# Down projection of parts 1 and 2 by seven products of weight quarters, with the weight sums made and stored ahead in part 1

## The chip, the cores and the metric

The kernel runs on one core of one Trainium2 chip. The metric is the time of one execution on the device in microseconds (us), as the median of several runs; lower is better. PE is the matrix engine (TensorE), DVE the vector engine, ACT the scalar engine, POOL the GpSimd engine, SP the engine that here only issues DMAs.

## What is computed

One layer of a hybrid decoder for 2048 prompt tokens and 32 sample tokens, in float32, with model width 1024 and inner width 2816 (11 x 256). What matters here is the feed-forward step:

```python
x = x + concat([h_mlstm, y_conv]) @ w_out
f = rmsnorm(x, g_ffn)
x = x + (silu(f @ w_gate) * (f @ w_up)) @ w_down     # w_down: 2816 x 1024
e = rmsnorm(pe @ w_ple, g_ple)
x = x + sigmoid(x @ w_pg) * e
```

## The kernel before

**Parts.** The 2080 tokens are worked through in three parts (q = 0, 1, 2) of 704, 704 and 672 tokens, each split in two token blocks of N = 352 or 336 columns. Every part reads every weight. A part runs the stages "in" (12 pairs of 256 output columns of w_in), "out" (4), the embedding, the feed-forward (11 pairs p of `gate` and `up`, 256 inner columns each), "pg" (4).

**Products.** A pair is a matrix of 1024 x 256 weights times 1024 x 2N activations, cut into quarters (A11, A12, A21, A22 of the weight, B11 and so on of the activations) and done by seven products instead of eight, P1 to P7, which use three of the quarters and four sums of weight quarters (S1 to S4) against four quarters and sums of the activations. Each product is 4 rows of 128 x 3 matmuls (12 in all), since a float32 product is made of high x high, high x low and low x high parts (`three`, L610). The order in a pair is P1 P6 P5 P7 P2 P4 P3. DVE and ACT add the products up from PSUM banks: P6 is added by DVE to a copy of P1 and frees its bank, which P7 needs; P7's addition frees the same bank for P4.

**Weight entries.** The weight operand of one product is an *entry*: 128 x 1024, the high part beside the low part, in one of five ring buffers (`RING`, `wring`). Entry e goes to the buffer of entry e - 5 and must wait until that has been used. An entry is either *prepared* from raw weights in SBUF (ACT copies the high part at L1287, POOL subtracts to get the low part at L2708) or *loaded* from the DRAM tensor `weight_parts` by a DMA that ACT issues (L1279). Part 0 prepares all entries, has DVE make the sums, and SP stores A11 and the sums of each pair (L1082); parts 1 and 2 load those five and prepare only A12 and A22. ACT, DVE and POOL call `ahead()` once per product, for the entry some four products later; each engine follows its own fixed program, in order, with semaphores between engines.

**Spares.** In part 0 the sums for "pg" (16 of them) are made in between as *spare* entries: SP loads a set of raw weights to `spare_raw` (L1091), DVE makes the four sums in place (`spare_sum`, L1753), ACT and POOL turn each into an entry of the ring, SP stores it, and PE passes over it. An entry of the ring that follows a spare by five waits until the spare has been stored.

**Raw weights.** SP loads raw weights two raws ahead into four buffers (`wraw`, `raw`, L1065), each when the raw four before has been prepared.

**Down.** `down(q, g)` (PE L980, DVE L2500) runs between `gate` and `up` of odd pairs and adds to x the product of the hidden pairs 2g - 1 and 2g with 512 rows of w_down, plainly: 16 products (8 output chunks of 128 by 2 token blocks) of 4 x 3 matmuls, banks 6 and 7 in turn, one DVE addition each (L2509). Its 8 entries are all prepared from raw weights. g = 0 has half a group, g = 5 the last pairs. The hidden values are split into high and low at L1580 (ACT) and L2443 (DVE): half c = 1 of a pair at its `up`'s end, half c = 0 after P1 of the next `gate`.

Of the kernel before, what the change touches and what calls it, by code (L numbers as in the profile page):

```python
# [168 lines left out]
def build(nc, x_prompt, x_sample, p_prompt, p_sample, state_C, state_n, state_m, state_conv, g_mix, w_in,  # L169
# [154 lines left out]

    def add_raw(pieces):

        r = len(raws)
# [20 lines left out]
    def add_spare(r, n):  # L348
# [6 lines left out]
        keep_entry(("pg", set_), name)  # L355
        spare_last[set_] = n_prepared[0]

    def add_pairs(q, of, members, order, spares):
# [5 lines left out]
        if stored:  # L364
            made = []
            for w, c0 in members:
                if (of[0], "A11") in kept_as:
# [4 lines left out]
                r, buf = add_raw([(slice(0, 1024), w[:, :, c0:c0 + P]), (slice(1024, 1536), w[:, 4:8, c0 + P:c0 + 2 * P])])  # L372
                v = buf[:, 0:1536].rearrange(k8, n=P)
                made.append((r, {"A11": v[:, 0:4, :], "A12": v[:, 4:8, :], "A22": v[:, 8:12, :]}, {}))
        else:
# [2526 lines left out]
```

## Time and profile before

| | |
|---|---|
| median of 3 runs | 2590.44 us (2589.56 to 2590.97) |
| the profiled execution | 2590.48 us, its span 2588.5 us |
| busy share of the span | PE 95%, weight loads 93%, DVE 58%, ACT 35%, POOL 39% |
| mean granted clock of TensorE | 0.985 of 2.4 GHz |
| DMA | 501 MB, 194 GB/s in the mean |

In the profile, a matmul's busy time overlaps the next one's, so busy PE means that matmuls follow each other; the pace of products is read from the start times of what they release. In the rows below, `<-` after a square bracket names what ended an engine's idle time. Feed-forward of part 1 runs from about 1240 to 1695 us, of part 2 from about 2080 to 2520 us.

### The profile page before, as it was taken

Reading aid. Unit: us, or ns where it says so; the run is one execution under the profiler, and the core shown is the slowest. Engines: PE = TensorE matmul, PEld = TensorE weight load, DVE = VectorE, ACT = ScalarE, POOL = GpSimd, SP = SyncE. Lnnn points to the kernel's source line nnn. Section 1 sums busy time; section 2 is a strip of 40 time slices with the busy share of each in tenths; the row PEclk is TensorE's granted clock in tenths of the full one; section 3 lists DMA queues with packets and bytes.
Section 4 is the critical chain, followed back from the end, with each engine's and each line's share of the span. In section 5 each row is a group of like instructions: output and inputs, shape, how many; then the busy total and the mean of one; then the engine's idle time right before and its main releaser. Section 6 shows DMA issues by size and latency. Waiting matters only on the chain.

```text
span 2588.5 us, 40956 instructions
## 1 busy us (share of the span) xinstructions
PE 2469.4 (95%) x15757; PEld 2404.5 (93%) x15757; DVE 1492.6 (58%) x2327; ACT 909.3 (35%) x1694; POOL 1011.0 (39%) x785
## 2 busy tenths in 40 slices
PE   7899788999999999999999999999999999999998
PEld 6888778999999989999999999998899999999997
DVE  7668987666555684477543333468457664332355
ACT  5344443343334543334312112355234431212133
POOL 4656755576666342122322122333222232322233
PEclk8999999999999999999999999999999999999999
DMA  6646644576666756575545544575657555564544
GB/s 222 218 174 236 221 150 179 192 272 220 213 229 210 228 158 205 174 268 160 179 163 195 200 142 163 179 225 179 196 183 244 184 182 171 187 219 164 173 137 149
DMA packets 285044, 501.00 MB, mean 194 GB/s; under 512 B 18428, under 2 KB 182613, under 8 KB 284343
## 3 DMA queue, kind: packets, MB, share of 16 engines
q1 hardware_dynamic: 212182, 273.59, 31.4%
q10 hardware_dynamic: 72672, 224.82, 26.2%
q8 instruction: 128, 2.10, 0.3%
q14 instruction: 62, 0.50, 0.1%
HBM read 374.70 MB, written 123.65 MB: 193 GB/s over the span
## 4 chain that ended last, share of the span: by engine, by line
PE 73%; DVE 7%; DMA 4%; issue 2%; ACT 1%; POOL 1%; DVEq 0%; ACTq 0%; POOLq 0%; SPq 0%
PE bank L612 23%; PE bank L614 22%; PE bank L613 22%; DMA wring<-weight_parts 2%; DVE qlo L1801 1%; DMA xs<-x_prompt 1%; PE bank L805 1%; DVE ess L2426 1%; PE bank L749 1%; PE bank L738 0%; POOL wring L2708 0%; DMA weight_parts<-wring 0%; PE bank L811 0%; DVE wraw L1791 0%; PE bank L727 0%
## 5 line engine op out<-in xcount | busy, mean ns | idle before, releaser
L2708 POOL TENSOR_TENSOR wring<-wraw,wring 128x512 fp32r<-128x512 f32 x525 | 768.1, 1472 | 1223.0 <-ACT wring L1287 1220.7
L612 PE MATMUL bank<-qhi,wring 128*128 128x352 f32 (+1 forms) x3540 | 1155.5, 326 | 65.2 <-DVE u L1912 13.9
L614 PE MATMUL bank<-qhi,wring 128*128 128x352 f32 (+1 forms) x3540 | 1139.5, 322 | 0.0
L613 PE MATMUL bank<-qlo,wring 128*128 128x352 f32 (+1 forms) x3540 | 1137.6, 321 | 0.0
L612 PEld LDWEIGHTS bank<-qhi,wring 128*128 128x128 f32 x3540 | 672.4, 190 | 89.7 <-issue 77.9
L613 PEld LDWEIGHTS bank<-qlo,wring 128*128 128x128 f32 x3540 | 672.4, 190 | 0.0
L614 PEld LDWEIGHTS bank<-qhi,wring 128*128 128x128 f32 x3540 | 670.0, 189 | 0.0
L1287 ACT ACTIVATE wring<-wraw 128x512 fp32r<-128x512 f32 x531 | 331.3, 628 | 710.3 <-PE bank L614 553.5
L612 PE MATMUL bank<-hid,wring 128*128 128x352 f32 (+1 forms) x1056 | 341.5, 323 | 12.4 <-DVE wide L2509 7.4
L614 PE MATMUL bank<-hid,wring 128*128 128x352 f32 (+1 forms) x1056 | 339.7, 322 | 0.0
L613 PE MATMUL bank<-hid,wring 128*128 128x352 f32 (+1 forms) x1056 | 338.9, 321 | 0.0
L2509 DVE TENSOR_TENSOR wide<-wide,bank 128x352 f32<-128x352 f32 (+1 forms) x288 | 148.0, 515 | 295.1 <-PE bank L614 295.1
L612 PEld LDWEIGHTS bank<-hid,wring 128*128 128x128 f32 x1056 | 199.9, 189 | 16.7 <-issue 13.0
L613 PEld LDWEIGHTS bank<-hid,wring 128*128 128x128 f32 x1056 | 200.8, 190 | 0.0
L614 PEld LDWEIGHTS bank<-hid,wring 128*128 128x128 f32 x1056 | 199.9, 189 | 0.0
L1862 DVE TENSOR_TENSOR u<-t,bank 128x352 f32<-128x352 f32 (+1 forms) x84 | 43.2, 514 | 187.0 <-PE bank L614 187.0
L2708 POOL TENSOR_TENSOR wring<-s,wring 128x512 fp32r<-128x512 f32 x74 | 109.3, 1489 | 64.0 <-ACT wring L1287 64.0
L1855 DVE TENSOR_TENSOR u<-t,bank 128x352 f32<-128x352 f32 (+1 forms) x87 | 44.6, 513 | 133.5 <-PE bank L614 104.4
L1580 ACT ACTIVATE hid<-sl 128x704 fp32r<-128x704 f32 (+3 forms) x69 | 52.1, 755 | 190.2 <-DVE sl L1833 183.4
L2443 DVE TENSOR_TENSOR hid<-sl,hid 128x704 fp32r<-128x704 f32 (+3 forms) x69 | 103.9, 1517 | 8.8 <-ACT hid L1580 7.4
L1316 ACT ACTIVATE t<-bank 128x352 f32<-128x352 f32 (+1 forms) x123 | 56.2, 457 | 129.8 <-PE bank L614 129.8
L1287 ACT ACTIVATE wring<-s 128x512 fp32r<-128x512 f32 x74 | 45.8, 629 | 87.6 <-PE bank L614 52.3
(322 smaller groups left out, 2413.3 us busy)
## 6 DMA issues: line engine op xcount, KB each, us to landing
wring<-weight_parts ACTq DMA_DIRECT2D x418, 512.0 KB, 4.5
weight_parts<-wring SPq DMA_DIRECT2D x201, 512.0 KB, 3.8
wraw<-w_down SPq DMA_DIRECT2D x33, 1024.0 KB, 8.3
wraw<-w_in SPq DMA_DIRECT2D x14, 1024.0 KB, 7.2
wraw<-w_gate SPq DMA_DIRECT2D x11, 1024.0 KB, 5.9
wraw<-w_up SPq DMA_DIRECT2D x11, 1024.0 KB, 6.0
wraw<-w_in SPq DMA_DIRECT2D x44, 256.0 KB, 5.2
wraw<-w_gate SPq DMA_DIRECT2D x44, 256.0 KB, 3.6
```

Of the source, the lines that this page charges most:

```text
L612: nc.tensor.matmul(o, hi, mh, start=begins, stop=False, skip_group_check=True)
L613: nc.tensor.matmul(o, hi, ml, start=False, stop=False, skip_group_check=True)
L614: return nc.tensor.matmul(o, lo, mh, start=False, stop=ends, skip_group_check=True)
L749: last = nc.tensor.matmul(bank[bk][:, a - a0:z - a0], roots[0:n, t:t + 1].to_broadcast([n, P]), ident[0:n, a - t0:z - t0], start=True, sto ...
L1287: nc.scalar.activation(whi[e % RING][:, :].rearrange("p (k n) -> p k n", k=k), w.src, ACT.Copy).then_inc(hi_done, 1)
L1316: nc.scalar.activation(t1[n % 2][:, 0:q.N], bank[a][:, 0:q.N], ACT.Copy).then_inc(free[a], 1)
L1580: nc.scalar.activation(hid[:, 0, x, blk], sl[:, c, blk], ACT.Copy).then_inc(h_hi, 1)
L1855: nc.vector.tensor_tensor(w2, t, c, add).then_inc(fc, 1)
L1862: nc.vector.tensor_tensor(w3, w2 if first else t, d, add).then_inc(fd, 1)
L2443: nc.vector.tensor_tensor(hid[:, 1, x, blk], sl[:, c, blk], hid[:, 0, x, blk], sub).then_inc(h_lo, 1)
L2509: last = nc.vector.tensor_tensor(x, x, bank[bk][:, 0:q.N], add)
L2708: nc.gpsimd.tensor_tensor(wlo[e % RING][:, :].rearrange(v, k=k), w.src, whi[e % RING][:, :].rearrange(v, k=k), ALU.subtract).then_inc(lo_d ...
```

## The change

The groups g = 1 to 4 of `down` in parts 1 and 2 are done by seven products of quarters too. Inner chunks of pair 2g - 1 against those of pair 2g are the rows, even against odd output chunks the columns of the quarters, token block 0 against 1 the columns of the activations. An entry now holds 2 x 2 chunks of weights (256 x 256), and half a group (a = 0 or 1, 512 output columns) has seven entries; each is used for two sets m of output chunks, 2 x 3 matmuls each, on all eight banks. Of the seven entries three are prepared from raw weights and four are loaded sums. The sums of the eight half groups (sets 4 to 11, 32 spares) are made in part 1 by the spares' machinery, in `up` 2 to `up` 8 (four each), `gate` 3 (two) and `down` 1 (two). The hidden pairs are kept in seven forms (B11, B12, B21, B22 and T1 to T4; high in `dhi`, low in `dlo_first`, `dlo_rest`), which takes more DVE and ACT passes per group; the raw buffers 2 and 3 give their room to them, so parts 1 and 2 have two raw buffers and SP loads a raw no longer two ahead. A cut of the diff:

```diff
+PG_SETS = 4
+DOWN_SEVEN = (1, 2, 3, 4)
+DOWN_SPARES = {("up", 2): {0: 16, 2: 17, 4: 18, 6: 19}, ("gate", 3): {4: 20, 6: 21}, ("down", 1): {1: 22, 3: 23},
+               ("up", 3): {0: 24, 2: 25, 4: 26, 6: 27}, ("up", 4): {0: 28, 2: 29, 4: 30, 6: 31},
...
+               ("up", 7): {0: 40, 2: 41, 4: 42, 6: 43}, ("up", 8): {0: 44, 2: 45, 4: 46, 6: 47}}
+DOWN_SPARE_LOADS = {25: 5, 27: 6, 29: 7, 31: 8, 35: 9, 37: 10, 41: 11}
...
+        b = r % 2 if q else r % RAW_RING
...
+            def down_by_sevens(q, g):
+                begins = ("P1", "P6", "P5", "P7", "P4")
+                for a in range(2):
+                    for name in DOWN_PRODUCTS:
...
+                        for m in range(2):
+                            first, second, third, fourth = DOWN_BANKS[m]
...
+                            for k in range(2):
+                                last = three(bank[bk][:, 0:q.N], hi[:, k, m, :], lo[:, k, m, :], dhi[:, op, k, 0:q.N],
+                                             down_low(op)[:, k, 0:q.N], name in begins and k == 0, k == 1)
...
                 for r in range(RAWS):
-                    raw()
+                    if q.n or r < RAWS - 2:
+                        raw()
...
+                    if q.n == 1 and r == 25:
+                        spare_weights(PG_SETS)
...
+                    if q.n == 1 and r in DOWN_SPARE_LOADS:
+                        spare_weights(DOWN_SPARE_LOADS[r])
...
+            def hidden_parts(q, p, c):
...
+                if p % 2:
+                    dve.wait_ge(h_hi, HID_HIGH[(q.n, p, (c, "B12"))])
+                    nc.vector.tensor_tensor(dlo_first[:, c, 0:q.N], u[:, 0], dhi[:, 0, c, 0:q.N], sub).then_inc(h_lo, 1)
+                    nc.vector.tensor_tensor(t_1, u[:, 1], u[:, 0], sub).then_inc(h_lo, 1)
+                    return
+                dve.wait_ge(h_hi, HID_HIGH[(q.n, p, (c, "B2"))])
+                nc.vector.tensor_tensor(dlo_rest[:, 0:2, c, 0:q.N], u, dhi[:, 1:3, c, 0:q.N], sub).then_inc(h_lo, 1)
...
+                nc.vector.tensor_tensor(t_2, u[:, 1], t_1, sub).then_inc(h_lo, 1)
+                nc.vector.tensor_tensor(t_3, u[:, 1], t_3, sub).then_inc(h_lo, 1)
...
+                nc.vector.tensor_tensor(t_4, u[:, 0], t_2, sub).then_inc(h_lo, 1)
```

Three places show how instructions move. In rows of the change, line numbers are those of the changed kernel (L1395 is the load L1279 of before, L1403 the ACT copy L1287).

**ACT, `up` 3 of part 1** (`wring` with a number is a ring buffer, `parts_kept` a stored part, `prod` a product of PE). Before, from the load for P1 of `up` to that for P1 of the next `gate`:

```order
L1279 DMA wring3_80<-weight_parts 128x1024 [waits parts_kept5,prod]
L1279 DMA wring4_81<-weight_parts 128x1024 [waits parts_kept1,prod]
L1279 DMA wring0_77<-weight_parts 128x1024 [waits parts_kept2,prod]
L1279 DMA wring1_78<-weight_parts 128x1024 [waits parts_kept4,prod]
L1287 ACTIVATE wring2_79<-wraw3_73 128x512 [waits landed3,prod]
L1316 ACTIVATE t1_1_114<-bank3 128x352 [waits free4,prod]
L1569 ACTIVATE sl_105<-sl_105 128x352 [waits free1]
L1287 ACTIVATE wring3_80<-wraw3_73 128x512 [waits prod]
L1279 DMA wring4_81<-weight_parts 128x1024 [waits parts_kept5,prod]
L1279 DMA wring0_77<-weight_parts 128x1024 [waits parts_kept0,prod]
```

Now, from the load for P6 of `up` to that for P1 of the next `gate`:

```order
L1395 DMA wring4_85<-weight_parts 128x1024 [waits parts_kept1,prod]
L1395 DMA wring0_81<-weight_parts 128x1024 [waits parts_kept2,prod]
L1403 ACTIVATE wring1_82<-spare_raw_78 128x512 [waits spare_sums,prod]
L1395 DMA wring2_83<-weight_parts 128x1024 [waits parts_kept4,prod]
L1403 ACTIVATE wring3_84<-wraw1_75 128x512 [waits landed1,parts_kept0]
L1403 ACTIVATE wring4_85<-spare_raw_78 128x512 [waits spare_sums,prod]
L1432 ACTIVATE t1_1_118<-bank3 128x352 [waits free4,prod]
L1700 ACTIVATE sl_109<-sl_109 128x352 [waits free1]
L1403 ACTIVATE wring0_81<-wraw1_75 128x512 [waits prod]
L1395 DMA wring1_82<-weight_parts 128x1024 [waits parts_kept5,parts_kept1]
L1403 ACTIVATE wring2_83<-spare_raw_78 128x512 [waits spare_sums,prod]
L1395 DMA wring3_84<-weight_parts 128x1024 [waits parts_kept0,prod]
```

The five buffers now also take the spares. The last load (P1 of `gate` 4) goes to buffer 3, which P2 of `up` held; between P2 and P1 PE has only P4 and P3. P7 (buffer 2) takes the place of P1, two products before it.

**DVE, from the end of an even pair's `up` into the next `gate`, part 2.** Before:

```order
L1831 TENSOR_TENSOR u2_115<-u2_115,bank4 128x336 [waits silu_done,free5,prod]
L1833 TENSOR_TENSOR sl_105<-sl_105,u2_115 128x336 [waits free4]
L2443 TENSOR_TENSOR hid_55<-sl_105,hid_55 128x672 [waits h_hi] x2
L1855 TENSOR_TENSOR u2_115<-t1_0_113,bank2 128x336 [waits h_raw,prod,free0]
L1862 TENSOR_TENSOR u3_116<-t1_0_113,bank2 128x336 [waits h_raw,prod]
```

Now (L2011 is L1855 of before, the addition of P6; L2018 is L1862, that of P7):

```order
L1987 TENSOR_TENSOR u2_119<-u2_119,bank4 128x336 [waits silu_done,free5,prod]
L1989 TENSOR_TENSOR sl_109<-sl_109,u2_119 128x336 [waits free4]
L2605 TENSOR_TENSOR dlo_rest_58<-sl_109,dhi_56 128x2x336 [waits h_hi]
L2607 TENSOR_TENSOR draw_59<-sl_109,draw_59 128x336 [waits h_lo]
L2608 TENSOR_TENSOR draw_59<-sl_109,draw_59 128x336
L2610 TENSOR_TENSOR draw_59<-sl_109,draw_59 128x336 [waits h_lo]
L2605 TENSOR_TENSOR dlo_rest_58<-sl_109,dhi_56 128x2x336 [waits h_hi]
L2607 TENSOR_TENSOR draw_59<-sl_109,draw_59 128x336 [waits h_lo]
L2608 TENSOR_TENSOR draw_59<-sl_109,draw_59 128x336
L2610 TENSOR_TENSOR draw_59<-sl_109,draw_59 128x336 [waits h_lo]
L2011 TENSOR_TENSOR u2_119<-t1_0_117,bank2 128x336 [waits h_raw,prod,free0]
L2617 TENSOR_TENSOR dlo_rest_58<-draw_59,dhi_56 128x2x336 [waits h_lo,h_hi] x2
```

Eight passes stand ahead of P6's addition where two stood.

**DVE and SP, `gate` 2 of part 1**, where the first set (set 4) comes in. DVE, from P6's addition (L2011) to P7's (L2018):

```order
L2011 TENSOR_TENSOR u2_119<-t1_0_117,bank2 128x352 [waits h_raw,prod,free0]
L2590 SCALAR_TENSOR_TENSOR wide0_49<-wide0_49,gains_131,bank7 128x352 [waits full7]
L2590 SCALAR_TENSOR_TENSOR wide0_49<-wide0_49,gains_131,bank7 128x352
L1919 TENSOR_TENSOR spare_raw_78<-spare_raw_78 128x4x128 [waits spare_in]
L2590 SCALAR_TENSOR_TENSOR wide0_49<-wide0_49,gains_131,bank7 128x352 x2
L2018 TENSOR_TENSOR u3_120<-t1_0_117,bank2 128x352 [waits h_raw,prod]
```

SP, from the raw of `gate` 3 to the load of set 5:

```order
L1181 DMA wraw0_74<-w_gate 128x4x128 [waits lo_done]
L1181 DMA wraw0_74<-w_gate 128x4x128
L1203 DMA spare_raw_78<-w_down 128x4x512 [waits full6,lo_done]
L1189 DMA weight_parts<-wring2_83 128x1024 [waits lo_done]
L1189 DMA weight_parts<-wring0_81 128x1024 [waits lo_done]
L1189 DMA weight_parts<-wring3_84 128x1024 [waits lo_done]
L1189 DMA weight_parts<-wring1_82 128x1024 [waits lo_done]
L1203 DMA spare_raw_78<-w_down 128x4x512 [waits lo_done]
```

The sum L1919 that waits for `spare_in` is new between the two additions. The load of set 5 stands behind the store of `up` 2's last spare; DVE's first sum of set 5 stands ahead of P3's additions of `up` 2.

## Rows read from the trace of the kernel before

**Rows 1.** The page's part 1, busy time by engine (us, share, instructions), and chain by engine:
```profile
PE 2469.4 (95%) x15757; PEld 2404.5 (93%) x15757; DVE 1492.6 (58%) x2327; ACT 909.3 (35%) x1694; POOL 1011.0 (39%) x785
PE 73%; DVE 7%; DMA 4%; issue 2%; ACT 1%; POOL 1%; DVEq 0%; ACTq 0%; POOLq 0%; SPq 0%
```

**Rows 2.** Waits of PE, 1274 to 1660 us (part 1): total us, times, longest:
```profile
PE bank L612 <- DVE hid L2443: 0.9, 1, 0.9
PE bank L612 <- DMA wring<-weight_parts: 0.6, 2, 0.5
```

**Rows 3.** Busy time by window: PE, PEld, DVE, ACT, POOL, clock, DMA share and GB/s:
```profile
1258.50:1272.00 13.50, 12.90 (x71) 12.89 (x72) 6.58 (x14) 0.00 (x0) 0.00 (x0) 0.87 0.41 123
1379.60:1393.10 13.50, 13.50 (x86) 13.50 (x85) 3.08 (x6) 3.40 (x7) 2.80 (x3) 1.00 0.78 273
622.00:636.00 14.00, 13.45 (x85) 13.20 (x84) 10.08 (x12) 6.46 (x11) 10.45 (x8) 1.00 0.92 317
1272.00:1658.00 386.00, 385.26 (x2411) 383.68 (x2409) 140.87 (x241) 83.27 (x142) 99.33 (x75) 1.00 0.53 177
```

**Rows 4.** Timeline, first and last addition of group 1, part 1 and part 2:
```profile
1333.73 0.52 DVE L2509 TENSOR_TENSOR wide<-wide,bank 128x352 f32<-128x352 f32 x1 [1.41 <-PE bank L614]
...
1362.38 0.52 DVE L2509 TENSOR_TENSOR wide<-wide,bank 128x352 f32<-128x352 f32 x1 [1.38 <-PE bank L614]
...
2172.09 0.50 DVE L2509 TENSOR_TENSOR wide<-wide,bank 128x336 f32<-128x336 f32 x1 [1.33 <-PE bank L614]
...
2199.73 0.50 DVE L2509 TENSOR_TENSOR wide<-wide,bank 128x336 f32<-128x336 f32 x1 [1.33 <-PE bank L614]
```

**Rows 5.** Timeline, DVE and POOL, from an `up` into a `gate`, part 2:
```profile
2321.65 1.48 POOL L2708 TENSOR_TENSOR wring<-wraw,wring 128x512 fp32r<-128x512 f32 x1 [9.05 <-ACT wring L1287]
2321.91 2.87 DVE L2443 TENSOR_TENSOR hid<-sl,hid 128x672 fp32r<-128x672 f32 x2
...
2324.48 1.45 POOL L2708 TENSOR_TENSOR wring<-wraw,wring 128x512 fp32r<-128x512 f32 x1 [1.35 <-ACT wring L1287]
2324.70 0.50 DVE L1855 TENSOR_TENSOR u<-t,bank 128x336 f32<-128x336 f32 x1
...
2328.30 0.51 DVE L1862 TENSOR_TENSOR u<-t,bank 128x336 f32<-128x336 f32 x1 [3.11 <-PE bank L614]
```

**Rows 6.** Timeline of DVE, part 1, one such pass that began with POOL idle:
```profile
1379.26 0.89 DVE L2443 TENSOR_TENSOR hid<-sl,hid 128x704 fp32r<-128x704 f32 x1 [0.56 <-ACT hid L1580]
```

**Rows 7.** Loads of stored parts, 1270 to 1660 us, and the time to landing:
```profile
L1279 ACTq DMA_DIRECT2D wring<-weight_parts x92: 326/326/327, 1270.5 to 1647.4; - x92
...
DMA to landing us min/median/max: 3.3/4.8/8.3
```

**Rows 8.** DMA issues: count, KB each, median us to landing; then landing of L1091:
```profile
wraw<-w_down SPq DMA_DIRECT2D x33, 1024.0 KB, 8.3
...
DMA to landing us min/median/max: 6.3/9.0/10.0
```

**Rows 9.** Groups of instructions, the spares of part 0 (mean ns behind the comma):
```profile
L2708 POOL TENSOR_TENSOR wring<-spare_raw,wring 128x512 fp32r<-128x512 f32 x16 | 22.9, 1429 | 19.1 <-ACT wring L1287 19.1
...
L1763 DVE TENSOR_TENSOR spare_raw<-spare_raw 128x512 f32<-128x512 f32 x16 | 15.3, 959 | 0.0
...
L1287 ACT ACTIVATE wring<-spare_raw 128x512 fp32r<-128x512 f32 x16 | 10.0, 624 | 25.5 <-PE bank L614 25.5
```

**Rows 10.** Timeline, `gate` 2 of part 1 (DVE, SP), and PE at 1259 us:
```profile
1259.10 0.40 PE L612 MATMUL bank<-hid,wring 128*128 128x352 f32 x1 [2.27 <-DVE wide L2509]
...
1294.48 0.37 SPq L1074 DMA_DIRECT2D wraw<-w_down  x1
...
1295.13 0.52 DVE L1855 TENSOR_TENSOR u<-t,bank 128x352 f32<-128x352 f32 x1 [1.82 <-PE bank L614]
1295.57 2.05 DVE L2434 SCALAR_TENSOR_TENSOR wide<-wide,gains,bank 128x352 f32<-128x352 f32 x4
1298.94 0.52 DVE L1862 TENSOR_TENSOR u<-t,bank 128x352 f32<-128x352 f32 x1 [1.32 <-PE bank L614]
```

More of the change, by code:

```diff
@@ L449, in build, with spares_of, add_down @@
     ALL4, ALL2 = slice(0, 4), slice(0, 2)
-    def add_down(g, n=None):
+    def spares_of(q, w, p):
+        return DOWN_SPARES.get((w, p)) if q == 1 else None
+    def add_down(q, g, n=None):
         if g == 0:
-            add_plain(w_down_v[:, 0:2, :], 2, D, [(ALL2, slice(256 * n, 256 * n + 256)) for n in range(4)])
+            add_plain(q, w_down_v[:, 0:2, :], 2, D, [(ALL2, slice(256 * n, 256 * n + 256)) for n in range(4)])
+            return
+        if down_seven(q, g):
+            spares = spares_of(q, "down", g) or {}
+            for a in range(2):
+                r, buf = add_raw(q, [(slice(0, 2048), w_down_v[:, 4 * g - 2:4 * g + 2, 512 * a:512 * a + 512])])
+                for j, p in enumerate(DOWN_PRODUCTS):
+                    name = WEIGHT_OF[p]
+                    if name in ("A11", "A12", "A22"):
+                        add_entry(r, by_quarters(buf)[name], 0, name == "A11")
+                        end[r] = n_prepared[0]
+                    else:
+                        n_loads[0] += 1
+                        entries.append(Entry(r, None, 0, False, None, None, kept_as[(("down", g - 1, a), name)]))
+                        entries[-1].loads = n_loads[0]
+                    if not a and j in spares:
+                        add_spare(r, spares[j])
             return
         for a in range(2):
-            add_plain(w_down_v[:, 4 * g - 2:4 * g + 2, 512 * a:512 * a + 512], 4, 512,
+            add_plain(q, w_down_v[:, 4 * g - 2:4 * g + 2, 512 * a:512 * a + 512], 4, 512,
                       [(ALL4, slice(P * j, P * j + P)) for j in range(4)], {1: n, 3: n + 1} if a and n is not None else None)
@@ L1282, in one_ahead @@
                 if w.first:
[L1283 removed]
+                    act.wait_ge(landed[raw_buffer[w.raw]], raw_landed[w.raw])
                 if w.total:
@@ L1565, in e_square, with down_by_sevens @@
                 nc.scalar.activation(esq[:, :, 0:q.T], q.U[:, 2 * x:2 * x + 2, 0:q.T], ACT.Square).then_inc(e_sq, 1)
+            def down_by_sevens(q, g):
+                n = PAIR_NO[(q.n, "up", 2 * g + 1)]
+                for a in range(2):
+                    for name in DOWN_PRODUCTS:
+                        ahead()
+                        if name != "P1":
+                            continue
+                        for m in range(2):
+                            bk, key = DOWN_BANKS[m][0], (q.n, "down", g, 2 * a + m)
+                            act.wait_ge(*written[key + ("P1",)])
+                            act.wait_ge(*drained[(q.n, "down", g, m, "P7") if a else PAIR_KEYS[n - 2 + m] + ("P3",)])
+                            nc.scalar.activation(t1[(n + m) % 2][:, 0:q.N], bank[bk][:, 0:q.N], ACT.Copy).then_inc(free[bk], 1)
+                            t_used[n + m] = key + ("P7",)
             def late_silu(q, p):
```

222 lines of the change are left out of this document (173 added, 49 removed), and 1 row of the table DOWN_SPARES.

## The prediction

> **What bounds the kernel now.** I read the busy shares and the chain first [rows 1]: PE is busy for 95% of the span and the chain of waits lies on PE for 73%. Then PE's waits in the feed-forward of part 1: in some 386 us PE waits 1.5 us in all, 0.6 us of it for loads of stored weights [rows 2]. DVE is busy 141 us of that window, POOL 99, ACT 83, and the DMA engines for 53% [rows 3]. So the stage is a nearly gapless stream of matmuls: a matmul taken out is a gain in full, and any new wait of PE is a loss in full. The question is what the new sums, stores and loads do to a ring of five buffers whose transfers only just fit now.
>
> The sum is made against the profiled execution, 2590.48 us (span 2588.5 and 2.0 around it), which is 0.04 above the median of the runs. About 0.2%, or 5.2 us, is what a measurement of this kernel can tell from no change.
>
> **The change, part by part.**
>
> *Matmuls removed.* A group took 16 x 12 = 192 matmuls and now takes 2 x 7 x 12 = 168. From the first to the last addition of a group are 15 steps of 12 matmuls: 28.65 us in part 1 and 27.64 in part 2 [rows 4], that is 0.1592 and 0.1536 us per matmul. Four groups a part, 24 each: 96 x 0.1592 = 15.3 us and 96 x 0.1536 = 14.7 us. Together -30.0 us.
>
> *DVE inside `down`.* Half a group has 18 additions where it had 8, 18 x 0.52 = 9.4 us [rows 4] in a half of 13.4 us (seven products of 1.91). They bunch up at P2 (six in one product), but each bank is wanted again only several products later. Zero; the cover is the rest of the half.
>
> *Hidden pairs, the odd boundary.* After an odd pair DVE makes four passes of half the length where it had two: zero.
>
> *Hidden pairs, the even boundary.* After an even pair eight passes stand ahead of P6's addition where there were two. In part 2 DVE starts them at 2321.91 and P6's addition follows at 2324.70; P7 of `gate` was written by 2328.30, so it began at 2328.30 - 1.84 = 2326.46, and needs the bank that this addition frees [rows 5]. A pass of 704 that begins with POOL idle takes 0.89 us [rows 6], so 0.85 for 672; a pass of 336 takes 0.51 by the length of the additions. The chain is 2 x (0.85 + 3 x 0.51) = 4.76 us undisturbed: P6's addition ends at 2321.91 + 4.76 + 0.50 = 2327.17, 0.7 us late. That is the lower end. The two passes of before took 2.87 instead of 1.70, 1.2 us lost beside POOL [rows 5]; I take the same loss, so 1.9 us late. If both POOL passes (1.48 and 1.45) came whole on top, it would be 3.6; that is the upper end. Four boundaries: +7.6 us in part 2 (2.8 to 14.4). In part 1 the next `gate`'s P1 is late by the item after this one, which moves the due time by about as much: zero, up to +6. The price of the upper end is what a rule says: the Trainium skill, "SBUF — State Buffer", section "Who interferes with whom", has a DVE instruction with two SBUF inputs and a GpSimd instruction that reads SBUF exclude each other for a whole instruction. By it the even boundaries of part 2 cost 14.4 us instead of 7.6; the rows show part of that loss.
>
> *The ring in `up` 2 to `up` 8 of part 1.* Now a load is issued when the product five entries back is done, with four products between: 4 x 1.91 = 7.6 us for a landing that takes 3.3 to 8.3, median 4.8 [rows 7]; hence the 0.6 us of waits. With four spares among an `up`'s seven products two loads, those of P7 and of the next `gate`'s P1, get a buffer that was freed only two products before: 3.8 us. ACT can't issue earlier, since it waits for that buffer in its program's order. PE then waits landing - 3.8: nothing at 3.3, 1.0 us at the median, 4.5 at the longest. P7 I take at the median, 1.0. P1 of `gate` is loaded beside the spare's store, the next raw and a set of 1 MB on SP's queue; I take 5.7, between median and longest, 1.9 us. Some 2.9 us an `up`, seven times: +20.3 us (ends 0 and 63; I use 8 to 35, since few of the 92 landings were near either end at once). `gate` 3 and `down` 1 with two spares each have one such load: +2 (0 to 4).
>
> *Set 4, DVE in `gate` 2.* The first sum of set 4 stands between P6's and P7's additions. SP issues the set after the raw of `gate` 3, which waits for `gate` 2's last preparation; that event was at 1294.48 [rows 10]. Two issues later, 1295.4, the load starts; 1 MB of w_down lands in 8.3 us in the median, the sets of part 0 took 6.3 to 10.0 [rows 8]. At 1303.7 DVE makes the sum (0.96 [rows 9]), two scalings (4 took 2.05) and P7's addition (0.52): 1306.2. P7 was written at 1298.94 and P4, one product later (1300.85), needs its bank: PE waits 5.4 us (3.4 to 7.1). After an idle time of 2.27 us the granted clock was 0.87 over 13.5 us [rows 3, 10], 1.8 us lost at the lower of the two levels (1.2 GHz); I add that once. +7.2.
>
> *Set 5, DVE at the end of `up` 2.* Its load waits for `up` 2's last spare, whose buffer P7 of `up` 2 frees, 8.0 us into the pair; ACT 0.62, POOL 1.43 [rows 9], then the store is issued: 10.2. Landed at 18.5, and only then come the sum (0.96), P3's two passes (1.05), the eight passes (4.9 undisturbed), the next sum (0.96) and P6's addition of `gate` 3 (0.52): 26.9. P7 of `gate` 3 is due after ten products and the ring's waits, 19.1 + 2.9 = 22.0. PE waits 4.9 us (2.9 to 9.5), and 1.8 for the clock: +6.7. The later sets have seven products more, or DVE asks for them after P6's addition: zero.
>
> *Raw weights.* SP now loads each raw behind the same preparation as before but for two raws later in the order, so 9 products or more (17 us) ahead of its use against 8.3 [rows 8]: zero.
>
> Sum: part 1 -15.3 + 20.3 + 2 + 7.2 + 6.7 = +20.9; part 2 -14.7 + 7.6 = -7.1. Together +13.8: **2604 us**.
>
> **The rivals.**
>
> *The loads land in time (faster).* If landings in the `up` pairs stay near 3.3 to 4.3, the ring costs 0.5 an `up`, 3.5, and 1 at `gate` 3; the sets at their quick end cost 3.4 and 2.9 with no loss of clock. Part 1: -15.3 + 10.8 = -4.5, part 2 -7.1: 2579 us. For it: a landing alone takes 3.3, and POOL, DVE and ACT have room. Against it: the median is 4.8 with the DMA engines 53% busy, and the spares add 16.8 MB of stores, 16.8 of loads and 8.4 of sets to 386 us at 177 GB/s, 110 MB in all, 286 GB/s. It decides from a cost of about 1.1 us an `up` on. 15%.
>
> *The gain and the waits cancel.* Costs between these: 2585 to 2596. 15%.
>
> *The DMA engines become the bound.* An `up` with spares moves five loads, its raw, four stores and a set, 6.3 MB, and a `gate` 3.1: 9.4 MB in 26.7 us. The densest window moved 317 GB/s at a share of 0.92, so 345 at the most [rows 3]: 27.3 us; at 317, 29.7 us. Then landings go to the long end, about 6 us an `up` instead of 2.9: 2604 + 22 = 2626. Against it: the halves of `down` between them move less. 24%. (The Trainium skill, "DMA: Bandwidth & Descriptors", section "Specifications", gives about 358 GB/s from HBM for a core; by it the 9.4 MB take 26.3 us and this rival would not hold.)
>
> *DVE and POOL exclude each other wholly.* The upper end at the even boundaries: 6.8 us more, 2611. Against it: the two passes of before lost 1.2 us, not 2.9 [rows 5]. The rule is the one named above. 10%.
>
> That the change doesn't do what it says is excluded by the order of the instructions: the spares and the 24 matmuls less a group stand there.
>
> **How the numbers follow.** The forecast has 36% (2596 to 2612). Slower by over 0.2% (above 2595.7) is the forecast, the DMA bound and the exclusion: 36 + 24 + 10 = 70%; within 0.2% 15%; faster 15%. The range 2584 to 2632 leaves out most of the faster rival's lower half and the far end of the DMA bound, about 2 in 10.
>
> **What would show it.** In part 2 `down` groups at 2 x 7 x 1.84 = 25.8 us instead of 29.5, and four waits of PE of about 2 us for the addition of P6 (L2011) at `gate` 3, 5, 7 and 9. In part 1 waits of PE or its weight load for `wring<-weight_parts` about 15 to 25 us in all, two waits of about 5 us behind L1919 at `gate` 2 and `gate` 3, a clock under 1 behind them. The forecast is wrong if PE's waits for loads stay under 8 us, or if part 2 doesn't gain.

## The result, and the profile after

The changed kernel takes 2622.89 us in the median of four runs (2615.56 to 2628.24), the kernel before beside it 2590.70 (2589.56 to 2599.69). The ratio is 1.0118, with an interval of 1.0103 to 1.0134: slower, by some 32 us where 13.8 were forecast; the time lies inside the stated range. The profiled execution is the slowest of the four, 2628.24 us with a span of 2626.5, so it shows 37.8 us to account for, 5.4 of them above the median.

The page of the changed kernel, busy time by engine and the chain [rows 1]:

```profile
PE 2460.2 (94%) x15565; PEld 2384.7 (91%) x15565; DVE 1649.9 (63%) x2615; ACT 955.8 (36%) x1790; POOL 1034.0 (39%) x801
PE 67%; DVE 9%; DMA 7%; issue 3%; POOL 1%; ACT 1%; DVEq 0%; SPq 0%; ACTq 0%; POOLq 0%
```

PE lost 9 us of busy time and 192 matmuls, and the chain has moved from PE (73% to 67%) to DVE and the DMAs. PE's waits, the first three rows in the feed-forward of part 1 [rows 2], 1285 to 1670 us, the last two in that of part 2, 2145 to 2530 us (total us, times, longest):

```profile
PE bank L696 <- DMA wring<-weight_parts: 19.4, 22, 2.9
PE bank L696 <- DVE u L2011: 11.1, 4, 9.0
PE bank L696 <- DVE u L2018: 5.8, 1, 5.8
...
PE bank L696 <- DVE u L2011: 6.3, 3, 2.3
PE bank L696 <- DMA wring<-weight_parts: 3.6, 2, 3.4
```

So 36.3 us of waits stand in part 1 where 1.5 stood. Windows of the same kernel (columns as in [rows 3]): all of that stretch, a stretch with spares from `up` 3 to `gate` 5, the densest 10 us, and 10 us each behind gate 2's wait, around gate 3's, around a late load in `down` 1, and behind the waits of gates 5, 7 and 9 in part 2:

```profile
1285.00:1670.00 385.00, 348.52 (x2087) 337.96 (x2086) 221.03 (x377) 105.61 (x188) 123.24 (x91) 0.97 0.78 268
1397.36:1443.67 46.31, 42.36 (x254) 40.03 (x253) 26.50 (x41) 15.51 (x27) 15.15 (x11) 1.00 0.93 323
1440.00:1450.00 10.00, 8.89 (x55) 8.34 (x54) 7.10 (x11) 4.05 (x6) 1.29 (x1) 1.00 1.04 391
1310.00:1320.00 10.00, 10.00 (x55) 9.94 (x54) 7.04 (x15) 3.32 (x6) 3.09 (x3) 0.85 0.48 159
1340.00:1350.00 10.00, 3.44 (x12) 3.47 (x13) 8.62 (x13) 1.84 (x3) 1.74 (x2) 0.51 0.30 105
1360.00:1370.00 10.00, 7.06 (x35) 6.76 (x34) 3.91 (x8) 2.60 (x5) 3.00 (x4) 0.83 1.01 386
2286.50:2296.50 10.00, 9.95 (x65) 9.98 (x66) 5.00 (x8) 4.05 (x9) 2.59 (x2) 1.00 0.82 273
2366.60:2376.60 10.00, 9.96 (x54) 9.99 (x55) 4.99 (x8) 3.12 (x6) 1.28 (x2) 0.83 0.83 260
2448.30:2458.30 10.00, 9.93 (x55) 9.96 (x56) 5.02 (x8) 3.16 (x6) 1.29 (x2) 0.83 0.79 253
```

DVE's busy time in part 1 went from 141 to 221 us, the traffic from 177 to 268 GB/s, and the granted clock shows 1.2 GHz for part of the time behind several waits.

**Where the time went.** The time of one pair is found by subtracting the starts of P7's addition (L1862 before, L2018 now) of equal pairs. From `up` 1 to `up` 10 of part 1 these go from 1282.17 to 1651.22 us before and from 1283.72 to 1688.83 now: 405.11 - 369.05 = +36.1 us. In part 2, 2122.50 to 2478.70 against 2161.13 to 2516.96: -0.4. The rest of the program adds 2. The same subtraction for all the kernels below:

| us against before | up 2 | gate 3 | up 3 to up 10 | part 1 | part 2 | whole time, median (before beside it) |
|---|---|---|---|---|---|---|
| changed kernel | 9.7 | 13.2 | 13.2 | 36.1 | -0.4 | 2622.89 (2590.70) |
| e1, P6's addition first | 9.2 | 11.5 | 14.6 | 35.4 | -11.1 | 2612.31 (2592.07) |
| e2, set 4 earlier | 1.9 | 13.3 | 12.2 | 27.4 | -0.2 | 2612.26 (2592.07) |
| e3, spares spread | 11.8 | 13.5 | 28.6 | 53.8 | -2.5 | 2635.11 (2592.07) |
| e4, raws alone | 0.0 | 0.0 | -1.6 | -1.6 | 0.5 | 2590.91 (2592.07) |
| e5, six buffers | 7.3 | 11.6 | 0.3 | 19.2 | -2.6 | 2606.23 (2591.97) |
| e7, six buffers, spread | 5.6 | 11.8 | 0.2 | 17.5 | -2.5 | 2606.43 (2592.35) |
| e6, e1 + e2 + e5 | 0.0 | 9.9 | 6.3 | 16.2 | -8.7 | 2594.63 (2591.97) |
| c2, sums in place, e1 | 0.0 | 2.9 | -6.8 | -3.9 | -11.1 | 2577.20 (2591.97) |
| c3, c2 with later passes | 0.0 | 1.5 | 2.1 | 3.6 | -10.7 | 2584.05 (2592.35) |

("up 2" is from `up` 1 to `up` 2, "gate 3" from there to `gate` 3, the next column from `gate` 3 to `up` 10.) What lies ahead of `up` 1 of part 1 has the same instructions in all the changed kernels, and ended between 4.8 us earlier and 1.6 later than before, so the stages tell more than the totals. Each stage is read from one execution: part 2 is the same program in the changed kernel, e2, e3, e5 and e7 and gives -0.2 to -2.6, so a difference of 2 us in one cell says little.

**The two sets.** The timeline of the changed kernel: DVE waits for set 4 in `gate` 2 and PE for DVE; then SP, DVE and PE around set 5 (L1203 loads a set, L1919 is a sum, L2605 to L2610 the eight passes, L2011 P6's addition):

```profile
1305.90 0.69 DVE L1919 TENSOR_TENSOR spare_raw<-spare_raw 128x512 f32<-128x512 f32 x1 [7.75 <-DMA spare_raw<-w_down]
1308.15 0.63 PE L696 MATMUL bank<-qhi,wring 128*128 128x352 f32 x1 [5.80 <-DVE u L2018]
...
1326.10 0.43 SPq L1203 DMA_DIRECT2D spare_raw<-w_down  x1
1326.57 0.72 SPq L1181 DMA_DIRECT2D wraw<-w_down  x1
1337.34 0.69 DVE L1919 TENSOR_TENSOR spare_raw<-spare_raw 128x512 f32<-128x512 f32 x1 [8.74 <-DMA spare_raw<-w_down]
1338.94 1.96 DVE L2605 TENSOR_TENSOR dlo_rest<-sl,dhi 128x704 fp32r<-128x704 f32 x1
1345.31 0.68 DVE L1919 TENSOR_TENSOR spare_raw<-spare_raw 128x512 f32<-128x512 f32 x1
1345.91 0.51 DVE L2011 TENSOR_TENSOR u<-t,bank 128x352 f32<-128x352 f32 x1
1346.56 0.63 PE L696 MATMUL bank<-qhi,wring 128*128 128x352 f32 x1 [9.01 <-DVE u L2011]
```

Set 5 took 11.2 us to land, with 1 MB of raw weights issued 0.5 us behind it, and DVE, in order, did nothing meanwhile; then the chain that the prediction named took 9.2 us to P7's first matmul, which needs the bank. Both waits are longer than the sum had them (5.80 against 5.4 us, 9.01 against 4.9).

**The even boundary.** DVE, POOL and PE from `up` 4 into `gate` 5 of part 2 [rows 5]:

```profile
2279.66 1.95 DVE L2605 TENSOR_TENSOR dlo_rest<-sl,dhi 128x672 fp32r<-128x672 f32 x1
2282.37 1.59 DVE L2610 TENSOR_TENSOR draw<-sl,draw 128x336 f32<-128x336 f32 x1
2283.89 0.85 DVE L2605 TENSOR_TENSOR dlo_rest<-sl,dhi 128x672 fp32r<-128x672 f32 x1
2285.50 0.50 DVE L2610 TENSOR_TENSOR draw<-sl,draw 128x336 f32<-128x336 f32 x1
2285.92 0.49 DVE L2011 TENSOR_TENSOR u<-t,bank 128x336 f32<-128x336 f32 x1
...
2279.41 1.49 POOL L2931 TENSOR_TENSOR wring<-wraw,wring 128x512 fp32r<-128x512 f32 x1 [9.03 <-ACT wring L1403]
2282.24 1.36 POOL L2931 TENSOR_TENSOR wring<-wraw,wring 128x512 fp32r<-128x512 f32 x1 [1.35 <-ACT wring L1403]
...
2286.55 0.39 PE L696 MATMUL bank<-qhi,wring 128*128 128x336 f32 x1 [2.29 <-DVE u L2011]
```

Two DVE passes begin just behind a POOL pass, and they take 1.95 us instead of 0.85 and 1.59 instead of 0.50: each POOL pass costs DVE 1.1 us here. PE waits 2.29 us, near the 1.9 of the sum.

### The profile page after: what moved, and what is told of

Read it like the earlier page. It is cut to its first block, busy times and chain, and to the rows that moved or that the text cites. A ratio compares the mean times of both kernels' runs of the same rounds, so it can differ in the third digit from the quotient of the medians.

```text
span 2626.5 us, 41349 instructions
## 1 busy us (share of the span) xinstructions
PE 2460.2 (94%) x15565; PEld 2384.7 (91%) x15565; DVE 1649.9 (63%) x2615; ACT 955.8 (36%) x1790; POOL 1034.0 (39%) x801
## 4 chain that ended last, share of the span: by engine, by line
PE 67%; DVE 9%; DMA 7%; issue 3%; POOL 1%; ACT 1%; DVEq 0%; SPq 0%; ACTq 0%; POOLq 0%
PE bank L696 21%; PE bank L698 20%; PE bank L697 20%; DMA wring<-weight_parts 4%; DMA weight_parts<-wring 1%; POOL wring L2931 1%; DVE qlo L1957 1%; DMA spare_raw<-w_down 1%; DVE dlo_rest L2605 1%; PE bank L889 1%; PE bank L822 1%; DVE ess L2582 1%; PE bank L833 0%; DVE draw L2607 0%; DMA xs<-x_prompt 0%
## 5 line engine op out<-in xcount | busy, mean ns | idle before, releaser
L2931 POOL TENSOR_TENSOR wring<-wraw,wring 128x512 fp32r<-128x512 f32 x509 | 746.8, 1476 | 1140.4 <-ACT wring L1403 1137.7
L1403 ACT ACTIVATE wring<-wraw 128x512 fp32r<-128x512 f32 x515 | 321.2, 628 | 610.5 <-PE bank L698 429.2
L696 PE MATMUL bank<-hid,wring 128*128 128x352 f32 (+1 forms) x544 | 177.8, 327 | 12.1 <-DVE wide L2732 7.1
L697 PE MATMUL bank<-hid,wring 128*128 128x352 f32 (+1 forms) x544 | 176.5, 324 | 0.0
L698 PE MATMUL bank<-hid,wring 128*128 128x352 f32 (+1 forms) x544 | 176.4, 324 | 0.0
L2732 DVE TENSOR_TENSOR wide<-wide,bank 128x352 f32<-128x352 f32 (+1 forms) x160 | 82.4, 516 | 119.8 <-PE bank L698 119.8
L696 PE MATMUL bank<-dhi,wring 128*128 128x352 f32 (+1 forms) x448 | 143.9, 321 | 3.0 <-DMA wring<-weight_parts 2.9
L2018 DVE TENSOR_TENSOR u<-t,bank 128x352 f32<-128x352 f32 (+1 forms) x84 | 43.2, 514 | 162.0 <-PE bank L698 162.0
L698 PE MATMUL bank<-dhi,wring 128*128 128x352 f32 (+1 forms) x448 | 143.8, 321 | 0.0
L2011 DVE TENSOR_TENSOR u<-t,bank 128x352 f32<-128x352 f32 (+1 forms) x87 | 44.5, 511 | 131.6 <-PE bank L698 82.0
L697 PE MATMUL bank<-dlo_rest,wring 128*128 128x352 f32 (+1 forms) x384 | 123.7, 322 | 0.0
L696 PEld LDWEIGHTS bank<-hid,wring 128*128 128x128 f32 x544 | 103.9, 191 | 16.3 <-issue 12.5
L2931 POOL TENSOR_TENSOR wring<-spare_raw,wring 128x512 fp32r<-128x512 f32 x48 | 66.4, 1383 | 117.3 <-ACT wring L1403 117.3
L697 PEld LDWEIGHTS bank<-hid,wring 128*128 128x128 f32 x544 | 103.9, 191 | 0.0
L698 PEld LDWEIGHTS bank<-hid,wring 128*128 128x128 f32 x544 | 103.9, 191 | 0.0
```

Source lines behind the costliest of these rows:

```text
L696: nc.tensor.matmul(o, hi, mh, start=begins, stop=False, skip_group_check=True)
L697: nc.tensor.matmul(o, hi, ml, start=False, stop=False, skip_group_check=True)
L698: return nc.tensor.matmul(o, lo, mh, start=False, stop=ends, skip_group_check=True)
L1403: nc.scalar.activation(whi[e % RING][:, :].rearrange("p (k n) -> p k n", k=k), w.src, ACT.Copy).then_inc(hi_done, 1)
L2011: nc.vector.tensor_tensor(w2, t, c, add).then_inc(fc, 1)
L2018: nc.vector.tensor_tensor(w3, w2 if first else t, d, add).then_inc(fd, 1)
```

## The experiments

**e1: P6's addition ahead of half of the passes.**

```diff
-                    if s == 0 and p:
+                    if p and s == (p % 2 and seven_pair(q.n, p - 1)):
                         hidden_low(q, p - 1, 0)
```

> P6's addition of an odd gate stands ahead of the four passes for half c = 0 of the even pair instead of behind them. My theory (P6's addition is late because eight passes of DVE stand ahead of it, and two POOL passes stretch them): PE's waits for that addition (L2011) at gate 5, 7 and 9 go from 2.0 to 2.5 us each to under 0.6 in part 2 and from 0.7 to 1.1 to zero in part 1; the time falls by 8 to 14 us from the changed kernel's 2622.9, to about 2611. Rival (DVE's work as a whole is too long for this stretch, so the wait only moves to the addition of P7 or to the loads that ACT issues behind the differences): under 4 us, 2619 or more.

2612.31 us, ratio 1.0086 (1.0072 to 1.0101). Its waits in part 2, in the same window as above:

```profile
PE bank L696 <- DMA wring<-weight_parts: 3.2, 6, 0.9
...
PE bank L696 <- DVE u L2011: 0.4, 1, 0.4
```

Part 2 gains 10.7 us, within the theory's 8 to 14, but only part of it is the theory's. 7.3 us of it stand behind `up` 3, where the waits for P6's addition at gates 5, 7 and 9 are gone. The other 3.5 stand at `gate` 3, where PE waits for a load in both kernels, 3.35 us in the changed kernel and 0.92 here; it is P1's load, issued at the same place, and landed 8.2 us after its issue in this execution instead of 10.6. The edit acts only behind P1, so this gain is not its doing (on these loads see e4). In part 1 the waits for P6's addition at gates 5, 7 and 9 go too, but longer waits for loads take their place and the sum of the part stays: there, not P6's addition alone, but the loads beside it bound the step. So the even boundary is what part 2 lost at gates 5, 7 and 9.

**e2: set 4 loaded one raw earlier.**

```diff
-                    if q.n == 1 and r == 25:
+                    if q.n == 1 and r == 24:
                         spare_weights(PG_SETS)
```

> SP issues the load of the first set (set 4) one raw earlier, behind the raw of up 2 instead of gate 3. My theory (DVE's sum between P6's and P7's addition of gate 2 waits for a load issued too late): the wait of 5.8 us for L2018 at gate 2 goes, and with it about 2.3 us at half clock behind it: 8 us less than the changed kernel, about 2615. The wait of 9 us at gate 3 stays, since set 5 is loaded behind set 4's last spare as before. Rival (transfers of this stretch are bound by the DMA engines, the wait turns up at another load): 0 to 3 us less.

2612.26 us, ratio 1.0080 (1.0063 to 1.0097). The wait for L2018 is gone from the rows of part 1, the one at gate 3 stays:

```profile
PE bank L696 <- DMA wring<-weight_parts: 18.4, 20, 2.4
PE bank L696 <- DVE u L2011: 12.2, 4, 9.8
```

The table has 7.8 us less up to `up` 2. So set 4 cost 8, wait and half clock together; that the load began some 10 us earlier cost nothing elsewhere.

**e3: the spares spread.**

```diff
-               ("up", 3): {0: 24, 2: 25, 4: 26, 6: 27}, ("up", 4): {0: 28, 2: 29, 4: 30, 6: 31},
...
+               ("up", 3): {2: 24, 3: 25, 6: 26}, ("gate", 4): {2: 27}, ("up", 4): {2: 28, 3: 29, 6: 30}, ("gate", 5): {2: 31},
...
+DOWN_SPARE_LOADS = {25: 5, 27: 6, 30: 7, 32: 8, 36: 9, 38: 10, 42: 11}
```

> The 24 spares of sets 6 to 11 stand behind P5, P7 and P3 of an up and P5 of the next gate (products 2, 3, 6 and 2) instead of behind P1, P5, P2 and P3 of the up. The transfers are the same in number and size, but no loaded entry has two spares among the four entries ahead of it any more, so every load is issued three or four products ahead (5.7 or 7.6 us). My theory (short lead): PE's waits for stored weights in up 3 to gate 9, some 16 us, fall to under 6, the time by 10 to 13 us, to about 2611. Rival (the DMA engines are the bound): the waits stay within 4 us of what they were, 2619 or more.

2635.11 us, ratio 1.0172 (1.0155 to 1.0189): 12 us slower than the changed kernel, where 12 faster was expected, and more than the rival said. Its waits in part 1, and ACT in `up` 3:

```profile
PE bank L696 <- DMA wring<-weight_parts: 25.1, 15, 3.8
PE bank L696 <- DVE u L2011: 19.6, 4, 9.7
```

```profile
1404.74 0.33 ACTq L1395 DMA_DIRECT2D wring<-weight_parts  x1
1405.19 0.50 ACT L1715 ACTIVATE dhi<-sl 128x352 fp32r<-128x352 f32 x1 [3.52 <-DMA weight_parts<-wring]
```

ACT is idle for 3.5 us until a store has landed and issues the load at 1404.74 only then. I had counted only how many products lie between a load and the buffer's last use. The ring has a second chain: the entry that follows a spare by five needs that spare's *store* landed (7.4 us here) before its own load may begin. With the old places this hits a loaded entry for two of the four spares, with mine for all four. And each set was asked for a product earlier than it landed (P7 waits 3.5 us for P6's addition at gates 5, 7 and 9). The runs e5 and e7 test this reading.

**e4: the raw buffers alone,** the kernel before with the change's rule for buffers and its order of loads.

```diff
+        b = r % 2 if part[0] else r % RAW_RING
...
-                    raw()
+                    if q.n or r < RAWS - 2:
+                        raw()
```

> The kernel before with two raw buffers instead of four in parts 1 and 2 and SP loading raws no longer two ahead, as in the changed kernel, and nothing else. My theory (term zero of the sum): within 2 us of before, 2588.5 to 2592.5. Rival (raws arrive late in the down groups, whose raws are 1 MB each): 4 to 12 us slower.

2590.91 us, ratio 0.9995 (0.9985 to 1.0004): the term was zero for the whole time, as the theory has it, but not everywhere. In `gate` 3 of part 2 this kernel lost 1.9 us. PE's wait there, then the time to landing of the four loads around it, in e4, in the kernel before and in the changed kernel, and the changed kernel's wait:

```profile
2159.34 0.42 PE L616 MATMUL bank<-qhi,wring 128*128 128x336 f32 x1 [1.67 <-DMA wring<-weight_parts]
DMA to landing us min/median/max: 8.2/8.9/9.2
DMA to landing us min/median/max: 5.3/6.3/7.3
DMA to landing us min/median/max: 9.5/10.0/10.6
2198.99 0.42 PE L696 MATMUL bank<-qhi,wring 128*128 128x336 f32 x1 [3.35 <-DMA wring<-weight_parts]
```

All three kernels have a small store of `m_sample` here, behind a raw that SP issues 0.5 to 1 us ahead of it. Before, this raw was 0.5 MB of w_up; with the new order of raws it is 1 MB of w_down, and the loads land later. How late differs from execution to execution (6.9 to 8.2 us in e1), but in every kernel of the table PE waits for a load in this gate, 0.9 to 3.4 us at the longest.

**e5: a sixth ring buffer in part 1.**

```diff
+    wring.append(at("wring5", [P, 1024], F32R, w0 + 16384))
...
+        b = (ring_of[-1] + 1) % (6 if six[0] <= e <= six[-1] else 5) if e else 0
+        ring_of.append(b)
+        ring_before.append(held.get(b))
```

> The changed kernel with a sixth ring buffer in the feed-forward of part 1 (the room of s1 and s2, which only part 0 needs there); entries, transfers and order stay. Theory A (a buffer too few: an entry may be loaded only when the product five entries back is done or the spare five entries back is stored, while the DMA engines have room): PE's waits for stored weights in part 1 fall from some 24 us to under 6 and the time by 14 to 18 us from the changed kernel's 2622.9, to about 2607. Theory B, the rival (the DMA engines are full between an up with spares and the next gate, where a landing takes 7 us instead of 4.8): the waits fall by less than 6 us, time 2617 or more. The two waits of DVE for sets 4 and 5 stay in both.

2606.23 us, ratio 1.0047 (1.0034 to 1.0060), 17 less than the changed kernel with all bytes and their order kept, as theory A has the time. The waits for loads in part 1 go from 19.4 to 10.7 us, more than theory B allows, but not under 6:

```profile
PE bank L704 <- DMA wring<-weight_parts: 10.7, 14, 1.5
```

**e7: six buffers and the spread spares.**

The edits of e3 and e5 together.

> The spread spares of e3 (up: behind products 2, 3 and 6; next gate: behind 2) with the sixth ring buffer of e5. Theory A (in e3 the entry that follows each spare by five was a load, so that the spare's store and that load, 5 to 7 us each, came one behind the other within five entries; a sixth buffer gives both a product more): waits for stored weights in part 1 fall from e3's 27 us to under 10. Theory B (the DMA engines are full in these stretches whatever the ring): they stay above 17 us. The waits of DVE for sets 4 and 5 and, at gate 5, 7 and 9, for sets that are asked for a product earlier than they land (3.5 us each in e3) stay in both; so about 2610 by A, 2622 or more by B.

2606.43 us, ratio 1.0054 (1.0036 to 1.0072): 29 us below e3, for one buffer. Its waits in part 1:

```profile
PE bank L704 <- DVE u L2019: 12.6, 4, 8.1
PE bank L704 <- DMA wring<-weight_parts: 6.3, 10, 1.5
```

(L2019 is P6's addition.) From 25.1 to 6.3 us of waits for the same transfers: the buffer count bounded the ring, in e3 by store and load in series. The DMA engines were nearly full, though. The window from `up` 3 to `gate` 5 in e5, where the changed kernel moved 323 GB/s at a share of 0.93:

```profile
1385.70:1431.40 45.70, 41.85 (x254) 40.09 (x253) 25.43 (x42) 15.41 (x27) 14.43 (x12) 1.00 0.97 340
```

This window is only 0.6 us shorter than that of the changed kernel. From `up` 3 to `gate` 5, `up` 5 to `gate` 7 and `up` 7 to `gate` 9 together, the stretches with the most transfers, the changed kernel took 16.7 us more than the kernel before, e5 11.5 and e7 11.2. So over two thirds of what the sixth buffer brought in e5 stand outside of them, and what holds the rest inside, full DMA engines or DVE's additions at the gates, was not separated.

**e6: the three mends together.**

The edits of e1, e2 and e5.

> The changed kernel with the three mends together: six ring buffers in part 1, set 4 loaded one raw earlier, P6's addition of an odd gate ahead of the four passes of half c = 0. If they add up: 2622.9 - 9 (set 4) - 11 (P6's addition in part 2) - 16 (ring) = 2587, within 5 us of the kernel before; the wait for set 5 at gate 3 stays at 8 to 10 us. Theory B: 2622.9 - 20 = 2603, with the waits for stored weights over 15 us still.

2594.63 us, ratio 1.0009 (0.9992 to 1.0026): level with the kernel before, and halfway between the two expectations. Waits for loads stay at 16.7 us in part 1, against 10.7 in e5: with most of the DVE waits gone, PE asks for the loads sooner (my reading, not tried). In e1's trace ACT also stands 1.9 us at `gate` 5 behind a copy of a difference that DVE makes later now, and issues the next load after that. Which of the two weighs more was not tried either. The mends do not add up.

**c2: sums in place, no spares.** DVE makes the sums of a half group in the down group of part 1 from its own raws; entries are used and stored.

```diff
-DOWN_SPARE_LOADS = {25: 5, 27: 6, 29: 7, 31: 8, 35: 9, 37: 10, 41: 11}
+DOWN_SPARES, DOWN_SPARE_LOADS = {}, {}
...
+                if q == 1:
...
+                    for j, n in zip((0, 1, 3, 6), turn):
+                        sums_at.setdefault(e0 + j, []).append((n, r, at_, where, turn, s1, s2))
+                    for n in names:
+                        add_entry(r, views[n], turn.get(n, 0), n == "A11")
+                        if n in turn:
+                            keep_entry(("down", g - 1, a), n)
```

> No spares in part 1 at all: there the four sums of a half group are made by DVE in the down group itself, from the raws that it loads anyway (S1 and S2 in s1 and s2, S3 and S4 in place), become entries, are used at once and stored for part 2. The 32 set loads and passed-over entries go (8.4 MB of sets, 16.8 MB of loads, and the ring keeps all its buffers for products). P6's addition as in e1. My theory (all of part 1's loss is made by the spares: ring, sets, DVE's waits): part 1 keeps its 15 us of matmuls and loses 0 to 4, part 2 as in e1 (11 us faster than before): about 2567 (2562 to 2577). Rival (in a half group DVE then has 18 additions, 9.4 us, and four sums of 0.7 to 1.7 us in 13.4 us, so that additions come late and PE waits for banks, or the second half's raw comes late for its first sum): 3 to 5 us lost per group, 2580 to 2587.

2577.20 us, ratio 0.9927 (0.9906 to 0.9948): faster than both kernels, at the far end of the theory's range. Its waits in part 1:

```profile
PE bank L707 <- DVE u L2027: 4.6, 4, 1.3
PE bank L707 <- DVE wide L2727: 3.1, 4, 0.8
...
PE bank L707 <- DMA wring<-weight_parts: 0.2, 1, 0.2
```

The waits for loads are gone; ring, sets and transfers left together, so this run doesn't tell them apart. The rival holds in part: some 3 us a group are lost to DVE, by P7's addition (L2027) and by additions of the down group (L2727), so that part 1 keeps 3.9 of its 15.3 us.

**c3: c2 with four passes one product later.**

```diff
-                    if s in (2, 3) and p % 2 and seven_pair(q.n, p - 1):
-                        for name in (("T1", "T2"), ("T3", "T4"))[s - 2]:
+                    if s in (3, 4) and p % 2 and seven_pair(q.n, p - 1):
+                        for name in (("T1", "T2"), ("T3", "T4"))[s - 3]:
```

> As the kernel with sums made in place, but the four passes for the low parts of T1 to T4 stand one product later in an odd gate: T1 and T2 behind P7's addition instead of ahead of it. If what is left in part 1 is P7's addition coming 1.2 us late at gate 3, 5, 7 and 9 (waits for L2027, 4.6 us in all), the waits go and the time falls by 4 to 6 us from that kernel's 2577.2, to about 2572. Rival (DVE's work has no room left there, so that the lateness moves to the additions of P5 and P2 and to the down group): within 2 us of it.

2584.05 us, ratio 0.9963 (0.9950 to 0.9976): 7 us slower than c2, where 4 to 6 faster was expected and the rival said within 2. The waits in part 1, and two windows behind the waits for L2721 of `down` 2 and `down` 4:

```profile
PE bank L707 <- DVE wide L2721: 7.0, 4, 1.9
PE bank L707 <- DVE wide L2727: 2.1, 3, 0.8
...
1425.00:1435.00 10.00, 8.14 (x39) 7.18 (x38) 9.11 (x16) 3.68 (x8) 6.69 (x5) 0.83 0.56 208
1595.00:1610.00 15.00, 12.56 (x59) 11.61 (x58) 11.89 (x21) 3.63 (x8) 8.28 (x6) 0.77 0.52 180
```

P7's wait is gone and a longer one stands at the additions of the down group: DVE has no room left there, as the rival said. Its size is more than that: the waits grow by some 2 us only, and 10 x 0.17 + 15 x 0.23 = 5.1 us are lost at 1.2 GHz behind two of them, where the clock of c2 stays at 1.00 in this stage.

## Why the prediction was right in sign and wrong in size

The sum had nearly every loss in its place and most of them too small. The step that failed most is the price of the even boundaries of part 2, +7.6 where those four gates lost 14.5: it left out the half clock behind waits of 2 us, and the raws' new order, put at zero, made loads late in the first of them. Next comes the landing of set 5, which took 11.2 us and not 8.3.

In part 1 the waits are taken from one matmul's start to the next, less 0.16 us for a matmul. Where the window behind a wait shows a clock under 1, half of the time at 1.2 GHz is put down to the clock.

- *Matmuls removed, -15.3 and -14.7:* right. `gate` 9 to `up` 9 of part 1, with group 4 and no wait, took 40.60 us instead of 44.00, 3.4 less for 24 matmuls. In part 2, without what gates 3, 5, 7 and 9 lost, the stage took 14.9 us less.
- *The ring, +22.3 with `gate` 3 and `down` 1:* the size was near, 23.6 us, in part by luck, and e5 shows that a sixth buffer takes 16.8 us off part 1. P7 of the ups cost 6.5 us where 7.0 were forecast, P1 of the next gates 8.3 where 13.3; the other 8.8 stand at P6 and P5, mostly of the gates, and in `down` 1 and 2, where 2 were forecast. The mechanism was half of it. The short lead is there: P7 of `up` 3 was loaded at 1390.32 and PE waited 1.00 us for it at 1395.15 (rows below). The store ahead of a load was in the order of the instructions and in my own words on the ring, and I put no price on it; e3 was built on that gap and failed.
- *Set 4, +7.2:* right, 8.3 (6.0 of wait and 2.3 of clock).
- *Set 5, +6.7:* 11.1, the upper end. The landing was taken at the median of the rows, 8.3 [rows 8]; it was 11.2. SP issues 1 MB of raws right behind it and ACT four loads around it, and that burst stood in the order that I had read; that it is the cause was not tried. The chain behind the landing took 9.2 us where 8.4 were forecast.
- *Even boundaries of part 1, zero:* 2.6 us at gates 5, 7 and 9. The zero rested on another delay moving the due time, P1 of the gate late by 1.9 us; that delay came, but with waits of 1.16, 1.20 and 1.15 us for P1's load it was too short to cover the chain.
- *Even boundaries of part 2, +7.6:* 14.5 at the four gates, the step that failed most. At gates 5, 7 and 9 it is 9.2 us where three times 1.9 were forecast. The waits were near the sum, 2.46, 2.28 and 2.05 from start to start against 1.9. What was left out is **the clock**: 0.83 over the 10 us behind gates 7 and 9 is 10 x 0.17 x 2 = 3.4 us at 1.2 GHz, 1.7 lost each time, in part after the gate's end. I had charged it for the waits of 5 us only, though [rows 3, 10] showed it behind 2.27 us.
- *Raw weights, zero:* the other half of that miss. `gate` 3 lost 5.3 us, not by its boundary: PE waited 3.35 us for a load, and the clock was 0.76 over the next 7 us, 1.7 lost. e4 has the raws' new order alone, and there the loads of this gate come late too (1.67 us of wait, where the kernel before has none). I had asked only whether each raw lands ahead of its own use, and not what 1 MB does to the loads issued beside it.
- *Clock behind `down` 1 of part 1, not in the sum:* a load there was 2.9 us late and 1.7 us more went at half clock (0.83 over the 10 us from 1360).

```profile
1390.32 0.34 ACTq L1395 DMA_DIRECT2D wring<-weight_parts  x1
...
1395.15 0.43 PE L696 MATMUL bank<-qhi,wring 128*128 128x352 f32 x1 [1.00 <-DMA wring<-weight_parts]
1395.41 0.32 PE L697 MATMUL bank<-qlo,wring 128*128 128x352 f32 x1
```

The differences in part 1 are 1.3 (ring), 1.7 (clock at `down` 1), 1.1 (set 4), 4.4 (set 5) and 2.6 (even boundaries); with 4.1 us more they make the 15 between +20.9 and +36.1. Most of these 4.1 stand behind the waits: the second matmul starts 0.26 us after the first (1395.15 and 1395.41), not 0.16, which makes some 2.6 us in 27 waits. Part 2 is 6.7 off, half of it the clock behind gates 7 and 9 and half `gate` 3.

Of the rivals, that DVE and POOL exclude each other wholly came true in its mechanism: both POOL passes delayed DVE, 1.1 us each, where I let one of them count. The Trainium skill, "SBUF — State Buffer", section "Who interferes with whom", has a DVE instruction with two SBUF inputs contend with a GpSimd instruction that reads SBUF, with the shared ports locked to one of them; the trace agrees, since the DVE passes that began during POOL's at 2279.41 and 2282.24 end 0.7 and 0.4 us after POOL's ends, and take 0.85 and 0.50 us when undisturbed. I had undisturbed passes too slow by 0.7 us in all (short ones start every 0.42 us, not 0.51), so that the wait came out near is in part luck. The DMA bound, at 2626 the nearest in time, doesn't explain the 17 us that a sixth buffer brings with the same bytes; in the three stretches with the most transfers, where 11.5 us stay lost in e5, it is not excluded.

## What to carry to other kernels

Where a ring holds both what is loaded and what is to be stored, count for each entry not only the products between its buffer's last use and its own, but the whole chain store, landing, load, landing, at the landings of a burst; entries that are made only to be stored are better made where they are also used (c2), or kept outside the ring (not tried). In a gapless stream, a wait of two microseconds is to be priced with the half clock that may stand behind it. A transfer that is moved is to be priced at the loads that it comes to stand beside, and not only at its own use. And an engine that does its work in order should not be made to wait for a transfer ahead of the one small addition that frees a bank.

## What the runs showed of the hardware that was not expected

The granted clock fell to 1.2 GHz for some 3.4 us after PE had been idle for 2.11 us (`gate` 7) and 1.88 us (`gate` 9), but not after 2.29 us (`gate` 5, 1.00 in the window above). In c3 it fell behind waits of 1.86 and 1.84 us at the additions of `down` 2 and `down` 4, the two windows shown. The densest 10 us moved 391 GB/s at a DMA share of 1.04, where I had taken 345 as the most from 317 at 0.92 [rows 3].
